# Cross-attention of sample tokens on four 32-column groups of the array, with eight cache slots

## The chip, the cores and the metric

The kernel runs on one core of one Trainium2 chip, all in float32 or float32r. The metric is the time of one execution on the device, in microseconds (us). TensorE is called PE here, VectorE DVE, ScalarE ACT, GpSimd POOL and SyncE SP.

## The reference

One layer of an encoder over 1024 prompt tokens (one sequence) and 8 x 16 sample tokens. The change touches the cross-attention of the sample tokens: each of the eight sequences has keys and values of its own, 256 memory tokens by four heads of 256.

```python
def mem_attention(q, mk, mv):
    s = jnp.einsum('bthd,bmhd->bhtm', q, mk.astype(q.dtype)).astype(jnp.float32) * (XA_DH ** -0.5)
    p = jax.nn.softmax(s, axis=-1).astype(q.dtype)
    return jnp.einsum('bhtm,bmhd->bthd', p, mv.astype(q.dtype))

def layer(x, ml_state, conv_buf, mk, mv, ...):
    xn = rms_norm(x, g_mix_pre)
    q, k, v, o, ig, fg, glu, xq, gates = jnp.split(xn @ w_in, IN_SPLITS, axis=-1)
    ...
    y_xa = mem_attention(xq.reshape(B, T, XA_HEADS, XA_DH), mk, mv).reshape(B, T, XA_W)
    mixed = (jax.nn.sigmoid(gates[..., 0:D_MODEL]) * (y_ml @ w_branch[0])
             + jax.nn.sigmoid(gates[..., D_MODEL:2 * D_MODEL]) * (y_cv @ w_branch[1])
             + jax.nn.sigmoid(gates[..., 2 * D_MODEL:]) * (y_xa @ w_branch[2]))
    x = x + rms_norm(mixed @ w_out, g_mix_post)
    ...
```

In the kernel the sample tokens are the last of nine tiles of 128 tokens: `mem_attention` runs on eight prompt tiles with one set of keys, then on the sample tile with eight.

## The kernel before, in words

The program is a sequence of phases, each written once for every engine: norms, the input projection, the projection of the convolution's branch, the mLSTM and its branch, the cross-attention (`sp_xattn`, `pe_xattn`, `act_xattn`, `dve_xattn`, `pool_xattn`) and its branch, and the FFN. Each engine runs its own list in order and waits on semaphores. Barrier 4 (`end_phase`) stands ahead of the cross-attention. The projection after it (L261, `pe_branch(pe, 2, xa_lo, 2 * NT)`) waits until POOL has written `A_lo` of all nine tiles (L1690).

Prompt tiles: for tile t PE computes scores (L1531, stationary queries, moving keys `mk_T`, two PSUM banks), DVE the maxima (L1701), ACT the exponentials with row sums (L1632), DVE scales by the reciprocal (L1708), PE transposes the probabilities (L1541), ACT copies them to `prob_T` (L1640), and PE multiplies with `mv` (L1550). SP loads the queries two tiles ahead (L1497), when the scores of the tile two before are done.

Sample tile, keys. The keys of sample b are loaded as rows of memory tokens into one of four slots of `cache_in` (L1484), so PE turns them by 16 transposes (`k_turn`, L1586) into four PSUM banks. ACT copies two of the banks (L1668) and DVE the other two (L1746) to one of two buffers `ck_T`, which lie on `mk_T` and `mv`. Then `k_scores` (L1596) multiplies: for each of 8 pieces of 128 columns the stationary operand is `xqm`, 128 columns of queries of which only the 16 of sample b are not zero, and the moving operand 256 columns of keys. All samples add into the same 128 x 1024 scores, head by head in columns. DVE makes `xqm` for each sample, by a clear (L1740) and a small copy (L1742).

```python
for k in range(KT):
    h = k // 2
    last = nc.tensor.matmul(PS[:, h // 2, MEM * (h % 2):MEM * (h % 2 + 1)], xqm[:, s, k], ck_T[s][:, k],
                            start=first and k % 4 == 0, stop=end and k % 4 == 3, skip_group_check=True)
```

Softmax of the sample tile: as for a prompt tile (L1701, L1632, L1708, L1541, L1640).

Sample tile, values. DVE makes for each sample a stationary operand `prob_own` (L1766 or L1764 clears, L1767 copies), again with 16 of 128 columns that are not zero, and PE multiplies it with the values of that sample (L1617), 8 matmuls of 256 moving columns. Then ACT copies the result (L1682), PE transposes it (L1623), DVE halves it into `xa_T` (L1717), ACT rounds it to `A_hi` (L1646) and POOL takes the rest to `A_lo` (L1690).

Loads. SP issues the keys of samples 0 to 3 behind the last query load, each later one when its slot has been turned; of the values SP issues samples 0, 2, 4, 6 and ACT 1, 3, 5, 7, each when its slot is free (`values`). Elsewhere the normaliser update of the mLSTM uses a stationary operand of 8 columns (L1256), which the prediction reads for comparison; L1252 ahead of it is full width.

## Time and profile before

| what | value |
|---|---|
| median of 3 runs | 2808.9 us (2807.84 to 2810.91) |
| the profiled execution, its time | 2810.57 us |
| the profiled execution, its span (first to last instruction) | 2808.8 us |
| mean granted clock of PE | 0.985 of 2.4 GHz |
| prompt tiles of the cross-attention | 1602.67 to 1673.5 us |
| keys, softmax, values of the sample tile | 1673.5 to 1755.0 us |
| first instruction of the projection behind it | 1761.45 us |

The profile is of one execution. Times in it count from the start of the span. "PE" rows are matmuls; "PEld" rows are loads of the stationary operand, which overlap them. A record of PE is longer than the distance to the next, since matmuls are pipelined: the distance from start to start is what one costs in a stream. A form such as 128\*8 128x256 says: 128 partitions by 8 stationary columns, 256 moving columns.

### The profile page before, as it was taken

Reading aid. Unit: us, or ns where it says so; the run is one execution under the profiler, and the core shown is the slowest. Engines: PE = TensorE matmul, PEld = TensorE weight load, DVE = VectorE, ACT = ScalarE, POOL = GpSimd, SP = SyncE. Lnnn points to the kernel's source line nnn. Section 1 sums busy time; section 2 is a strip of 40 time slices with the busy share of each in tenths; the row PEclk is TensorE's granted clock in tenths of the full one; section 3 lists DMA queues with packets and bytes.
Section 4 is the critical chain, followed back from the end, with each engine's and each line's share of the span. In section 5 each row is a group of like instructions: output and inputs, shape, how many; then the busy total and the mean of one; then the engine's idle time right before and its main releaser. Section 6 shows DMA issues by size and latency. Waiting matters only on the chain.

```text
span 2808.8 us, 37457 instructions
## 1 busy us (share of the span) xinstructions
PE 2686.7 (96%) x15080; PEld 2566.7 (91%) x15080; DVE 1087.8 (39%) x1334; ACT 625.3 (22%) x912; POOL 650.2 (23%) x332
## 2 busy tenths in 40 slices
PE   5899999999999999899998898999999999999998
PEld 5899999999999999898888887988999998989897
DVE  3320199999962222216643342245220211110115
ACT  4331111111113233204521141024211110201021
POOL 5421212222221211221201120140313231404131
PEclk9999999999999999999999999999999999999999
DMA  6422333334252223244565534442202020202013
GB/s 180 144 88 88 106 129 121 110 108 142 91 186 80 96 79 105 98 160 106 135 209 177 175 130 147 163 137 90 75 23 68 29 63 23 68 16 68 13 40 135
DMA packets 286828, 294.96 MB, mean 105 GB/s; under 512 B 11386, under 2 KB 250322, under 8 KB 286704
## 3 DMA queue, kind: packets, MB, share of 16 engines
q1 hardware_dynamic: 271800, 239.91, 27.6%
q10 hardware_dynamic: 14912, 53.48, 4.8%
q8 instruction: 75, 1.23, 0.2%
q14 instruction: 41, 0.34, 0.0%
HBM read 208.27 MB, written 85.55 MB: 105 GB/s over the span
## 4 chain that ended last, share of the span: by engine, by line
PE 49%; issue 39%; POOL 8%; DVE 2%; ACT 1%; DMA 1%; SPq 0%; POOLq 0%; DVEq 0%; ACTq 0%
PE PS L1966 19%; PE PS L261 11%; PE PS L1989 9%; POOL w_lo L253 7%; PE PS L1936 3%; PE PS L1531 1%; PE PS L1550 1%; PE PS L1206 1%; PE PS L1214 1%; PE PS L1172 1%; DVE x_T L536 0%; PE PS L1179 0%; DVE y_T L1369 0%; DMA stage<-in_state_conv 0%; PE PS L1167 0%
## 5 line engine op out<-in xcount | busy, mean ns | idle before, releaser
L261 PE MATMUL PS<-A_hi,w_hi 128*128 128x384 f32 x2496 | 573.4, 336 | 17.3 <-DVE A_lo L935 10.0
L261 PE MATMUL PS<-A_lo,w_hi 128*128 128x384 f32 x2496 | 570.9, 335 | 0.0
L261 PE MATMUL PS<-A_hi,w_lo 128*128 128x384 f32 x2496 | 570.4, 335 | 0.0
L253 POOL TENSOR_TENSOR w_lo<-w_raw,w_hi 128x1024 fp32r<-128x1024 f32 x120 | 306.1, 2554 | 1052.6 <-ACT w_hi L249 1052.6
L261 PEld LDWEIGHTS PS<-A_hi,w_hi 128*128 128x128 f32 x2496 | 446.4, 188 | 20.1 <-issue 17.0
L261 PEld LDWEIGHTS PS<-A_lo,w_hi 128*128 128x128 f32 x2496 | 446.5, 188 | 0.0
L261 PEld LDWEIGHTS PS<-A_hi,w_lo 128*128 128x128 f32 x2496 | 446.2, 188 | 0.0
L890 DVE SCALAR_TENSOR_TENSOR c_out<-ext,taps,c_out 128x1024 f32<-128x1024 f32 x480 | 424.1, 962 | 0.7 <-DVE c_out L890 0.7
L249 ACT CAST w_hi<-w_raw 128x1024 fp32r<-128x1024 f32 x120 | 126.3, 1053 | 1079.2 <-PE PS L261 1071.8
L1966 PE MATMUL PS<-A_hi,w_hi 128*128 128x384 f32 x1056 | 242.5, 334 | 2.8 <-POOL w_lo L1881 2.8
L1966 PE MATMUL PS<-A_lo,w_hi 128*128 128x384 f32 x1056 | 242.3, 334 | 0.0
L1966 PE MATMUL PS<-A_hi,w_lo 128*128 128x384 f32 x1056 | 242.2, 334 | 0.0
L1966 PEld LDWEIGHTS PS<-A_hi,w_hi 128*128 128x128 f32 x1056 | 188.2, 188 | 3.5 <-POOL w_lo L1881 3.1
L1966 PEld LDWEIGHTS PS<-A_lo,w_hi 128*128 128x128 f32 x1056 | 188.4, 188 | 0.0
L1966 PEld LDWEIGHTS PS<-A_hi,w_lo 128*128 128x128 f32 x1056 | 188.4, 188 | 0.0
L1881 POOL TENSOR_TENSOR fo_lo<-w_raw,fo_hi 128x1024 fp32r<-128x1024 f32 x22 | 52.9, 2404 | 412.9 <-ACT fo_hi L1876 412.9
L1881 POOL TENSOR_TENSOR w_lo<-w_raw,w_hi 128x1024 fp32r<-128x1024 f32 x44 | 106.2, 2415 | 151.4 <-ACT w_hi L1876 151.4
L2162 DVE SCALAR_TENSOR_TENSOR vb<-vb,PS 128x1152 f32<-128x1152 f32 x22 | 29.8, 1354 | 272.8 <-ACT vb L2043 272.8
L1989 PE MATMUL PS<-fo_hi,G_hi 128*128 128x512 f32 x396 | 122.7, 391 | 0.0
L1989 PE MATMUL PS<-fo_lo,G_hi 128*128 128x512 f32 x396 | 122.0, 389 | 0.0
L1989 PE MATMUL PS<-fo_hi,G_lo 128*128 128x512 f32 x396 | 122.0, 389 | 0.0
L2173 DVE TENSOR_TENSOR Y_tok<-Y_tok,PS 128x1024 f32<-128x1024 f32 x45 | 54.9, 1221 | 153.6 <-PE PS L1989 153.0
(289 smaller groups left out, 2766.3 us busy)
## 6 DMA issues: line engine op xcount, KB each, us to landing
proj_d<-stage ACTq DMA_DIRECT2D x80, 576.0 KB, 2.7
w_raw<-in_w_in SPq DMA_DIRECT2D x80, 512.0 KB, 4.2
w_raw<-in_w_ffn_in SPq DMA_DIRECT2D x44, 512.0 KB, 3.9
w_raw<-in_w_branch SPq DMA_DIRECT2D x24, 512.0 KB, 4.3
w_raw<-in_w_ffn_out SPq DMA_DIRECT2D x22, 512.0 KB, 3.4
glu<-proj_d SPq DMA_DIRECT2D x16, 576.0 KB, 5.9
gate_in<-proj_d SPq DMA_DIRECT2D x16, 576.0 KB, 6.4
part_d<-part_out SPq DMA_DIRECT2D x16, 576.0 KB, 4.7
```

What stands on the lines that cost most here:

```text
L249: nc.scalar.copy(w_hi[:, s % SPLIT, 0:kt], w_raw[:, s, 0:kt]).then_inc(w_hi_done, 1)
L253: nc.gpsimd.tensor_tensor(w_lo[:, s % SPLIT, 0:kt], w_raw[:, s, 0:kt], w_hi[:, s % SPLIT, 0:kt].bitcast(F32), ALU.subtract).then_inc(w_lo_ ...
L261: last = nc.tensor.matmul(out, w[:, k], m(k, c), start=start and k == 0 and n == 0, stop=stop and k == kt - 1 and n == 2)
L890: steps.mark(nc.vector.scalar_tensor_tensor(out=c, in0=src, scalar=tap_scalar(w, k), in1=c, op0=ALU.mult, op1=ALU.add))
L1172: last = nc.tensor.matmul(PS[:, 0, P * h:P * (h + 1)], k_in[:, b, 2 * h + z], q_in[:, b, 2 * h + z], start=z == 0, stop=z == 1)
L1206: last = nc.tensor.matmul(PS[:, 4 + h, 0:E1], q_in[:, b, 2 * h + z], C_T[:, h, z], start=z == 0, stop=z == 1)
L1881: nc.gpsimd.tensor_tensor(l_, job_raw(n), h_.bitcast(F32), ALU.subtract).then_inc(w_lo_done, 1)
L1936: last = nc.tensor.matmul(PS[:, b + z], m_, w_[:, k, 512 * z:512 * (z + 1)], start=k == 0 and n == 0, stop=k == KT - 1 and n == 2)
L1966: last = nc.tensor.matmul(PS[:, 3 * (u % 2) + c, 0:TC], w_[:, u % 2, k], m_[:, k, TC * c:TC * (c + 1)], start=k == 0 and n == 0, stop=k == ...
L1989: last = nc.tensor.matmul(PS[:, b + z], g_[:, k, P * t:P * (t + 1)], w_[:, k, 512 * z:512 * (z + 1)], start=k == 0 and n == 0, stop=k == C ...
L2162: nc.vector.scalar_tensor_tensor(out=thirds(vb[:]), in0=thirds(vb[:]), scalar=1.0, in1=PS[:, 0:3, 0:TC], op0=ALU.add, op1=ALU.mult).then_i ...
L2173: nc.vector.tensor_tensor(Y_tok[:, t], Y_tok[:, t], pair(fo_banks(t)), ALU.add).then_inc(y_acc, 1)
```

## The change

Rows and columns of the sample tile's scores are laid out anew. Before, row 16b + r was token r of sample b, and the columns held the four heads. Now the row is 32h + 16e + r for head h and sample 2p + e, and the columns hold the four pairs p of samples, 256 for each. A matmul for sample b and head h has 32 stationary columns, of which 16 are zero (those of the other sample of the pair), and writes PSUM partitions 32h to 32h + 31; the program gives it the array tile of 128 rows by 32 columns at column 32h. In the order of the program, heads take turns.

- `own_q`, the queries of all eight samples, lies over both buffers of `prob_T` and is made once, by a clear of 2048 columns (L1719 of the changed kernel) and two copies. `own_p`, the probabilities, lies over both buffers of `prob` and is made once, by a clear of 2048 columns (L1734) and four copies (L1738).
- There are eight slots for keys and values: four of `cache_in` and four new ones (`cache_more`). Key b is loaded behind the query load of prompt tile b + 2, so during the prompt tiles. Value b is loaded into slot b when its keys have been turned, all by SP.
- The loops over samples are written out. The last transposes and the halving follow the new layout.
- Semaphores of the mLSTM phase are used again, so POOL clears them before barrier 4 instead of behind it.

```diff
-        cache_loaded = [sem(f"cache_loaded{s}") for s in range(4)]
...
+        ml_sems.close()
+        cache_loaded = [sem(f"cache_loaded{s}") for s in range(NB)]
...
-        prob_own = prob[:].rearrange("p b h m -> p b (h m)").rearrange("p b (m h j) -> p b m h j", m=2, h=H)
+        own_q = prob_T[:].rearrange("p a m h j -> p (a m h j)").rearrange("p (b k r) -> p b k r", b=NB, k=KT)
+        own_p = prob[:].rearrange("p b h m -> p (b h m)").rearrange("p (m b h r) -> p m b h r", m=2, b=NB, h=H)
...
+        cache_more = [nc.alloc_sbuf_tensor_at(f"cache_more{n}", [P, 2, D], F32, offset=x) for n, x in enumerate((201600, 209792, 217984, O_GATE))]
...
         def sp_xattn(sp):
...
+            for t in range(2, NPT + 1):
+                load_xq(sp, t, t % 2)
+                cache(sp, "cache_mem_k", t - 2)
+            cache(sp, "cache_mem_k", NB - 1)
+            for b in range(NB):
+                sp.wait_ge(ck_turn, 2 * (b + 1))
+                cache(sp, "cache_mem_v", b)
...
+            def k_scores(b):
                 pe.wait_ge(ck_a, b + 1)
                 pe.wait_ge(ck_d, b + 1)
-                pe.wait_ge(ck_q, b + 1)
-                for k in range(KT):
-                    h = k // 2
-                    last = nc.tensor.matmul(PS[:, h // 2, MEM * (h % 2):MEM * (h % 2 + 1)], xqm[:, s, k], ck_T[s][:, k],
-                                            start=first and k % 4 == 0, stop=end and k % 4 == 3, skip_group_check=True)
+                pe.wait_ge(ck_q, 1)
+                p = b // 2
+                for z in range(2):
+                    for h in range(H):
+                        last = nc.tensor.matmul(PS[32 * h:32 * (h + 1), p // 2, MEM * (p % 2):MEM * (p % 2 + 1)], own_q[:, b, 2 * h + z],
+                                                ck_T[b % 2][:, 2 * h + z], start=b % 4 == 0 and z == 0, stop=b % 4 == 3 and z == 1,
+                                                skip_group_check=True)
                 last.then_inc(ck_used, 1)
...
+            pe.wait_ge(cv_own, 1)
             for b in range(NB):
-                pe.wait_ge(cv_own, b + 1)
-                pe.wait_ge(cache_loaded[b % 4], 16 * (NB // 4 + b // 4 + 1))
...
+                pe.wait_ge(cache_loaded[b], 32)
+                p = b // 2
+                for m in range(2):
+                    for h in range(H):
+                        last = nc.tensor.matmul(PS[32 * h:32 * (h + 1), 6 + p // 2, DH * (p % 2):DH * (p % 2 + 1)], own_p[:, m, b, h],
+                                                slot_of(b)[:, m, DH * h:DH * (h + 1)], start=b % 4 == 0 and m == 0,
+                                                stop=b % 4 == 3 and m == 1, skip_group_check=True)
                 last.then_inc(cv_used, 1)
...
+            dve.wait_ge(xa_y, NPT)
+            nc.vector.memset(own_q, 0.0).then_inc(sq_zero, 1)
+            dve.wait_ge(sq_zero, 1)
+            for e in range(2):
+                last = nc.vector.tensor_copy(
+                    own_q.rearrange("p (g e) k r -> p g e k r", e=2)[:, :, e, :, TS * e:TS * (e + 1)],
+                    xq_in[:, 0].rearrange("p k (g e r) -> p g e k r", e=2, r=TS)[:, :, e])
+            last.then_inc(ck_q, 1)
...
             dve.wait_ge(xa_copied, SB + 1)
...
+            nc.vector.memset(own_p, 0.0).then_inc(sq_zero, 1)
+            dve.wait_ge(sq_zero, 2)
+            for e in range(2):
+                for m in range(2):
+                    last = nc.vector.tensor_copy(
+                        own_p.rearrange("p m (g e) h r -> p m g e h r", e=2)[:, m, :, e, :, TS * e:TS * (e + 1)],
+                        prob_T[:, 0, m].rearrange("p g (h e r) -> p g h e r", e=2, r=TS)[:, :, :, e])
+            last.then_inc(cv_own, 1)
...
             pool_branch(pool, 1)
+            clear_mlstm(pool)
             end_phase(pool, 4)
-            clear_mlstm(pool)
```

The order of PE's instructions at the end of the keys, the softmax and the values, before (the last rows of the loop over samples, then what follows; "x64" is 64 matmuls of the program; the shape is that of the output):

```order
L1586 MATMUL PS<-ident,cache_in 128x128 x16
L1596 MATMUL PS<-mk_T,prob_T 128x256 x8
L1603 REGISTER_ALU
L1603 COMPARE_AND_BRANCH
L1596 MATMUL PS<-mv,prob_T 128x256 x8
L1541 MATMUL PS<-ident,prob 128x128 x8
L1617 MATMUL PS<-cache_in,prob 128x256 x64
L1623 MATMUL PS<-ident,prob_T 128x128 x8
```

and in the changed kernel:

```order
L1574 MATMUL PS<-ident,cache_more_54 128x128 x16
L1585 MATMUL PS<-mk_T,prob_T 32x256 x8
L1585 MATMUL PS<-mv,prob_T 32x256 x8
L1529 MATMUL PS<-ident,prob 128x128 x8
L1604 MATMUL PS<-cache_in,prob 32x256 x32
L1604 MATMUL PS<-cache_more_51,prob 32x256 x8
L1604 MATMUL PS<-cache_more_52,prob 32x256 x8
L1604 MATMUL PS<-cache_more_53,prob 32x256 x8
L1604 MATMUL PS<-cache_more_54,prob 32x256 x8
L1611 MATMUL PS<-ident,prob_T 128x128 x8
```

The matmuls are as many as before and stand in the same places; each writes 32 partitions, not 128.

The order of DVE's instructions from the last sample's key copy to the last halving, before:

```order
L1746 COPY mv<-PS 128x1024
L1751 REGISTER_ALU
L1751 COMPARE_AND_BRANCH
L1701 TENSOR_REDUCE smax<-PS 128x4
L1706 RECIPROCAL rsum<-ssum 128x4
L1708 TENSOR_SCALAR prob<-prob,rsum 128x256 x4
L1766 MEMSET prob 128x1024
L1767 COPY prob<-prob_T 128x8x16
L1766 MEMSET prob 128x1024
L1767 COPY prob<-prob_T 128x8x16
L1764 MEMSET prob 128x8x16
L1767 COPY prob<-prob_T 128x8x16
```

and in the changed kernel:

```order
L1730 COPY mv<-PS 128x1024
L1681 TENSOR_REDUCE smax<-PS 128x4
L1686 RECIPROCAL rsum<-ssum 128x4
L1688 TENSOR_SCALAR prob<-prob,rsum 128x256 x4
L1734 MEMSET prob 128x2048
L1738 COPY prob<-prob_T 128x4x4x16 x4
L1746 TENSOR_SCALAR xa_T<-PS 128x2x128 x4
```

All eight operands are now made ahead of the first value matmul, where one was.

The order of SP's transfers around the cross-attention, before:

```order
L1497 DMA xq_in<-proj_d 128x8x128 [waits xa_S]
L1484 DMA cache_in<-in_cache_mem_k 128x2x1024 x4
L1515 UNCONDITIONAL_BRANCH
L1484 DMA cache_in<-in_cache_mem_k 128x2x1024 [waits ck_turn] x4
L1515 REGISTER_ALU
L1515 COMPARE_AND_BRANCH
L1484 DMA cache_in<-in_cache_mem_v 128x2x1024 [waits ck_turn] x2
L1484 DMA cache_in<-in_cache_mem_v 128x2x1024 [waits cv_used] x2
```

and in the changed kernel:

```order
L1494 DMA xq_in<-proj_d 128x8x128 [waits xa_S]
L1489 DMA cache_more_52<-in_cache_mem_k 128x2x1024
L1494 DMA xq_in<-proj_d 128x8x128 [waits xa_S]
L1489 DMA cache_more_53<-in_cache_mem_k 128x2x1024
L1489 DMA cache_more_54<-in_cache_mem_k 128x2x1024
L1489 DMA cache_in<-in_cache_mem_v 128x2x1024 [waits ck_turn] x4
L1489 DMA cache_more_51<-in_cache_mem_v 128x2x1024 [waits ck_turn]
L1489 DMA cache_more_52<-in_cache_mem_v 128x2x1024 [waits ck_turn]
```

Key loads now alternate with the query loads, and no value load waits for a value matmul.

## Rows read from the trace of the kernel before

**Rows 1.** The page, busy time and share of the span by engine.

```profile
PE 2686.7 (96%) x15080; PEld 2566.7 (91%) x15080; DVE 1087.8 (39%) x1334; ACT 625.3 (22%) x912; POOL 650.2 (23%) x332
```

**Rows 2.** Windows by stretch: us, busy of each engine (instructions), clock, DMA share, GB/s.

```profile
1608.00:1649.60 41.60, 40.25 (x271) 36.93 (x270) 20.52 (x45) 20.99 (x61) 9.71 (x8) 1.00 0.27 77
1649.60:1673.50 23.90, 20.62 (x164) 19.41 (x162) 9.72 (x20) 10.80 (x26) 7.96 (x7) 1.00 0.51 198
1673.50:1716.10 42.60, 42.18 (x256) 37.85 (x256) 19.11 (x26) 8.77 (x10) 2.52 (x2) 1.00 0.56 198
1716.10:1725.40 9.30, 2.01 (x9) 1.64 (x9) 3.69 (x8) 2.94 (x9) 0.00 (x0) 0.64 0.00 0
1725.40:1755.00 29.60, 29.58 (x128) 25.41 (x128) 3.49 (x14) 0.00 (x0) 0.00 (x0) 0.94 0.41 142
1755.00:1761.50 6.50, 1.14 (x9) 0.91 (x9) 1.29 (x2) 2.23 (x3) 2.48 (x2) 0.86 0.00 0
```

**Rows 3.** Groups by line and shape, 1673.5 to 1761.4 us: busy, mean ns | idle before.

```profile
L1617 PE MATMUL PS<-cache_in,prob 128*128 128x256 f32 x128 | 29.6, 396 | 2.6 <-issue 2.6
...
L1586 PE MATMUL PS<-ident,cache_in 128*128 128x128 f32 x128 | 15.5, 274 | 1.7 <-DVE xa_T L1717 1.4 <-ACT mk_T L1668 0.3
L1596 PE MATMUL PS<-mk_T,prob_T 128*128 128x256 f32 x64 | 14.5, 379 | 0.0
...
L1746 DVE COPY mv<-PS 128x1024 f32<-128x1024 f32 x4 | 4.9, 1223 | 0.3
```

**Rows 4.** Timeline of PE in the keys: start us, us, engine, line.

```profile
1677.78 3.62 PE L1596 MATMUL PS<-mk_T,prob_T 128*128 128x256 f32 x16
...
1681.23 1.91 PE L1586 MATMUL PS<-ident,cache_in 128*128 128x128 f32 x16
...
1682.98 3.62 PE L1596 MATMUL PS<-mv,prob_T 128*128 128x256 f32 x16
```

**Rows 5.** Timeline of the softmax of the sample tile and the first value operand.

```profile
1719.59 1.14 DVE L1708 TENSOR_SCALAR prob<-prob,rsum 128x256 f32<-128x256 f32 x4
...
1724.08 0.91 DVE L1766 MEMSET prob<- 128x1024 f32 x1 [3.35 <-ACT prob_T L1640]
1725.03 0.23 DVE L1767 COPY prob<-prob_T 128x128 f32<-128x128 f32 x1
```

**Rows 6.** Timeline of PE in the last normaliser update of the mLSTM.

```profile
1478.85 1.03 PE L1252 MATMUL PS<-Cb_T,qm 128*128 128x257 f32 x4
1479.81 1.89 PE L1256 MATMUL PS<-kw,own 128*8 128x256 f32 x8
```

**Rows 7.** Windows of two us at the start of the values, PE alone.

```profile
1726.00:1728.00 2.00, 2.00 (x6) 0.50 0.00 0
1728.00:1730.00 2.00, 2.00 (x9) 0.77 0.00 0
```

**Rows 8.** DMA: windows of a query load and of key loads; landing of four key loads.

```profile
1624.00:1632.00 8.00, 8.00 (x58) 7.54 (x57) 3.75 (x8) 4.06 (x11) 2.59 (x3) 1.00 0.24 68
1656.00:1664.00 8.00, 7.51 (x61) 6.94 (x61) 3.81 (x8) 4.37 (x12) 2.64 (x3) 1.00 0.82 338
...
DMA to landing us min/median/max: 6.2/9.0/11.9
DMA to landing us min/median/max: 3.9/4.1/9.0
```

**Rows 9.** Timeline of DVE at the end of the prompt tiles.

```profile
1673.67 0.91 DVE L1740 MEMSET prob_T<- 128x1024 f32 x1 [0.16 <-issue]
...
1674.62 0.51 DVE L1742 COPY prob_T<-xq_in 128x128 f32<-128x128 f32 x1
...
1675.57 1.23 DVE L1746 COPY mk_T<-PS 128x1024 f32<-128x1024 f32 x1 [0.44 <-PE PS L1586]
```

**Rows 10.** Timeline of a prompt tile: query loads and scores.

```profile
1608.22 41.35 SPq L1497 DMA_DIRECT2D xq_in<-proj_d  x7
...
1613.78 3.62 PE L1531 MATMUL PS<-mk_T,xq_in 128*128 128x256 f32 x16
```

More of the change, by code:

```diff
@@ L1603, in pe_xattn @@
-            with pe.Fori(1, NB // 4) as i:
-                for s in range(4):
-                    b = 4 * i + s
-                    k_turn(b, s, i)
-                    k_scores(b - 1, 1 - s % 2)
-            k_scores(NB - 1, 1, end=True)
+                pe.wait_ge(ck_q, 1)
[5 more added lines that the diff above has]
+                                                skip_group_check=True)
@@ L1609, in pe_xattn @@
+                last.then_inc(ck_used, 1)
+            k_turn(0)
+            for b in range(1, NB):
+                k_turn(b)
+                k_scores(b - 1)
+            k_scores(NB - 1)
+            pe.wait_ge(ck_a, NB)
             p_turn(SB, 0)
             pe.wait_ge(xa_copied, SB + 1)
+            pe.wait_ge(ck_d, NB)
+            pe.wait_ge(cv_own, 1)
             for b in range(NB):
-                pe.wait_ge(cv_own, b + 1)
-                pe.wait_ge(cache_loaded[b % 4], 16 * (NB // 4 + b // 4 + 1))
@@ L1615, in pe_xattn @@
-                for h in range(H):
-                    for m in range(2):
-                        last = nc.tensor.matmul(PS[:, 6 + h // 2, DH * (h % 2):DH * (h % 2 + 1)], prob_own[:, b % 2, m, h],
-                                                cache_in[:, b % 4, m, DH * h:DH * (h + 1)], start=b == 0 and m == 0 and h % 2 == 0,
-                                                stop=b == NB - 1 and m == 1 and h % 2 == 1, skip_group_check=True)
+                pe.wait_ge(cache_loaded[b], 32)
+                p = b // 2
@@ L1662, in act_xattn @@
             hi(NPT - 1)
-            def keys(b, s):
+            for b in range(NB):
                 act.wait_ge(ck_turn, 2 * b + 1)
-                if not isinstance(b, int) or b > 1:
+                if b > 1:
                     act.wait_ge(ck_used, b - 1)
-                nc.scalar.copy(ck_T[s][:, 0:4].rearrange("p (a k) m -> p a (k m)", a=2), PS[:, 4:6]).then_inc(ck_a, 1)
-            keys(0, 0)
-            keys(1, 1)
-            with act.Fori(1, NB // 2) as i:
-                for s in range(2):
-                    keys(2 * i + s, s)
-            for b in (1, 3):
-                values(act, b)
+                nc.scalar.copy(ck_T[b % 2][:, 0:4].rearrange("p (a k) m -> p a (k m)", a=2), PS[:, 4:6]).then_inc(ck_a, 1)
             act.wait_ge(ck_used, NB)
@@ L1678, in act_xattn @@
             turned(SB, 0)
-            for b in (5, 7):
-                values(act, b)
             act.wait_ge(cv_used, NB)
+            act.wait_ge(cv_own, 1)
             nc.scalar.copy(xa_nat, PS[:, 6:8].rearrange("p n c -> p (n c)")).then_inc(cv_nat, 1)
@@ L1759, in dve_xattn @@
             dve.wait_ge(xa_copied, SB + 1)
[L1760 to L1768 removed]
+            nc.vector.memset(own_p, 0.0).then_inc(sq_zero, 1)
[6 more added lines that the diff above has]
+            last.then_inc(cv_own, 1)
+            dve.wait_ge(cv_turned, 1)
+            for n in range(2):
+                dve.wait_ge(xa_lo, 2 * SB + n - 1)
+                for z in range(2):
+                    last = nc.vector.tensor_scalar(xa_T[:, n].rearrange("p (h z) (g r) -> p z h g r", z=2, r=32)[:, z],
+                                                   PS[:, 6 + z].rearrange("p (g h r) -> p h g r", h=H, r=32)[:, 2 * n:2 * n + 2], 0.5, None, ALU.mult)
+                last.then_inc(xa_half, 1)
         early_sems.close()
[L1772 removed]
         U_F = U_BR + 3 * KT
```

86 lines of the change are left out of this document (19 added, 67 removed).

## The prediction

> **What bounds it now.** I read the page first: PE is busy 96% of the span [rows 1], so what counts is where PE works longer than it must, or waits. The windows then cut the cross-attention into stretches [rows 2]: eight prompt tiles (1608 to 1673.5), the keys of the eight samples (1673.5 to 1716.1), the softmax of the sample tile (to 1725.4), the values (to 1755.0) and the way back to the next projection (to 1761.5). Keys and values take 42.6 + 29.6 us, and PE is busy in 42.18 and 29.58 of them, so both stretches end when PE ends, and DVE and ACT are covered there. In the softmax stretch PE works 2.01 of 9.3 us: there each DVE and ACT step is on the path.
>
> The groups by line say what PE does [rows 3]. A sample's keys are 16 transposes and 8 score matmuls, its values 8 matmuls. 64 score matmuls stand as 2 x 64 records (one group for each buffer of keys; one is shown) and 64 value matmuls as 128: an f32 matmul goes through the array in two passes. In the timeline [rows 4] one sample's 16 passes run from 1677.78 to the next instruction at 1681.23: 3.45 us, 216 ns a pass, and the 16 transposes from 1681.23 to 1682.98: 1.75 us. So keys cost 5.2 us and values 3.46 us a sample, whatever share of the 128 stationary columns is zero.
>
> **The array.** Each matmul now has 32 stationary columns and writes partitions 32h to 32h + 31; the count stays 8 + 8 a sample with 256 moving columns each. The nearest rows are the eight passes of L1256, with 8 stationary columns [rows 6]: 1.89 us from first start to last end, 7 x 216 + 379 ns. A narrow matmul alone is therefore not shorter; all gain must come from passes in different column groups that run at once. No row here shows two passes at once, so the bounds are 16 slots of 216 ns a sample (none overlaps) and 4 slots (all four groups at once). I take the middle, 8 slots: the two passes of one matmul have the same 32 columns and follow one another in the stream, so the second has to wait for the first; if passes start in program order, what can overlap is the second pass of head h with the first pass of head h + 1, two at a time.
> - Values: 128 passes in 64 slots, 13.8 us in place of 27.65: **13.8 gained**.
> - Keys: 8 slots and one for the last lone pass are 1.94 us in place of 3.46.
>
> The Trainium skill, "TensorE: Matmul & The Clock Gate", part 3 on packing small matmuls, says that matmuls stay in program order and that three column tiles at once measured 2.38 times as fast; no run so far shows it here. By that figure alone the 55.3 us of scores and values would fall to an estimated 23 us, between my middle and the lower bound.
>
> **Changes of array shape.** Full-width transposes and narrow matmuls alternate in the keys, 14 changes that cost anything. The trace has the change: the last of four L1252 passes starts 3 x 216 ns after 1478.85, at 1479.50, the next was due at 1479.72 and came at 1479.81 [rows 6]: 0.1 us. Bounds are nothing and 163 ns (the 379 of a record less the slot of 216). I take 0.1: 1.4 us. The Trainium skill, "TensorEngine Tiling (Array Packing)", key properties, says that a change of tiling mode drains TensorE; the 0.1 us gap agrees.
>
> **Keys, put together.** At the end of the prompt tiles DVE cleared 1024 columns (0.91 us), copied 128 queries, and was idle till the first keys came at 1675.57 [rows 9]. Now it clears 2048 (1.82) and makes two copies of 512. A four-pack of 256-column operations runs in 1.14 us [rows 5], 0.285 each, so I take 0.57 a copy. The first key copy then starts at 1673.67 + 1.82 + 1.14 + 0.1 = 1676.7, 1.1 us late, and the second half of the next transposes waits for it: the first scores start at 1677.78 + 1.1 + 0.1 = 1679.0. From there 8 x 1.94 + 6 x 1.75 + 1.4 = 27.4 us, end 1706.4 instead of 1716.1: **9.7 gained**. The six other clears and small copies that leave DVE were covered by PE; they gain nothing. DVE's key copy of 1.22 us [rows 3] has 1.94 + 0.87 us of PE beside it. If scores took 0.87 us, DVE would be nearly level, which costs 0.4 us once, at the last sample.
>
> **Softmax.** The same instructions up to prob_T. Then a clear of 0.91 and a copy of 0.23 [rows 5] stood before the first value matmul; now it is a clear of 2048 columns (1.82) and four copies of 256 (4 x 0.285 = 1.14, between 4 x 0.23 and 4 x 0.35): **1.9 lost**, since PE waits for the last copy. The seven later operand builds ran beside 3.46 us of PE each and gain nothing. The halving at the end is four operations of 256 columns for two of 512: **0.1 lost**.
>
> **Clock.** PE idles in the softmax, and its granted clock falls to 0.50 (1.2 GHz); the first values run so until about 1729.5, when it returns to 1.0 [rows 7]. Values took 29.6 us for 27.65 of work, so the fall costs 2 us. PE idles there as before or longer, so the same 2 us stays, in each case below.
>
> **Loads.** Each key load of 1 MB now goes behind a query load on SP's queue, one per prompt tile. A query tile takes 0.24 of 8 us, 1.9 us of the engines; at 338 GB/s the share was 0.82, so 1 MB takes about 2.6 us. 4.5 us a tile stand against 7.9. Four key loads issued together landed after 6.2 to 11.9 us [rows 8], one after the other, so a query load waits for one key load at most, 2.6 us on top of its 4.1. From the third prompt tile on it has over 7 us to spare (issue at the end of the tile two before); the one for tile 2, issued at 1608.2, lands before the first key load: PE wanted it at 1613.78 [rows 10]. Nothing, at worst 1 us. Value loads are issued at each sample's transposes, the last near 1703, and needed from 1718: hidden. The four that ACT issued move to SP, which waits for nothing else there. POOL's clear of semaphores is done before the barrier, while SP still waits for stores: nothing.
>
> **Sum.** 9.7 + 13.8 - 1.9 - 0.1 = 21.5 us. The profiled execution took 2810.57 us (its span is 2808.8), 1.7 above the median of the runs; 2810.57 - 21.5 = 2789.1, and against the median of 2808.9 it is **2787.4 us**. Its own range, with the change of shape at 0 to 163 ns and an overlap somewhat better or worse than pairs, is 2782 to 2794.
>
> **Rivals.**
> - *All four groups at once.* Scores 0.87 us a sample: 7.0 + 10.5 + 1.4 + 0.4 from 1679.0 is 1698.3, 17.8 gained; values 6.9 for 27.65, 20.7 gained; less 2.0: 36.5, **2772.4 us**. For it: the heads stand in turn in the stream. Against: each stands there as two passes of one group. The 2.38 of the page named above lies on this side. 15%.
> - *No overlap.* Keys 8 x 3.46 + 10.5 + 1.4 = 39.6 from 1679.0, 2.5 lost; values even; 2.0 lost in softmax and end: 4.5 lost, **2813.4 us**, 0.16%. For it: no row shows two passes at once, L1256 least of all, though its passes are of one group. 20%.
> - *Slower: a change of column group costs like a change of shape.* Passes do not overlap and each of the 128 matmuls goes to another group than the one before; at the 0.1 us of rows 6 that is 12.8 us more: **2826 us**. It decides from 10 ns a change on (1.2 us over 128). Against: at full width each pass takes another stationary operand, and its 216 ns are 256 columns at two cycles of 2.4 GHz (213 ns) with no room for such a cost [rows 4]. 10%.
> - *Late queries.* The key loads delay each of seven query loads so that a tile waits 2 us: 14 us given back, **2801 us**. Against: 4.5 of 7.9 us. 5%.
>
> **How the numbers follow.** Pairs 47%, four 15%, none 20%, slower 10%, late queries 5%, the rest mixtures. About 0.2%, 5.6 us, is what a measurement can tell from no change. Faster 0.70; without overlap the loss is so near 0.2% that its 20% is split: same 0.16, slower 0.14. Pairs and four hold 62%, so the range must reach to no overlap as well: 2770 to 2815.
>
> **What would show it.** Right: value passes 108 ns apart on average, a sample's scores 1.9 us, the values over in 16 us with the first 4 us at half clock; first scores 1.2 us later than before; a clear of 1.8 us before the values. Wrong: passes still 216 ns apart (no overlap), 54 ns (four), PE idle between samples with DVE or a load named, query waits in the prompt tiles, or a stretch of 7.9 us a tile that has grown.

## The result, and the profile after

The changed kernel takes **2778.1 us** (median of 4 runs, 2776.85 to 2779.18) against 2808.4 for the kernel before in 4 runs of the same session: a ratio of 0.989, 95% interval 0.9873 to 0.9907. The profiled execution took 2779.18 us (span 2777.4), 31.4 less than that of before. The forecast was 2787.4, with 2770 to 2815: the direction and the range hold, the size does not, for 21.5 us were forecast.

The page, busy time and share of the span by engine, answers to [rows 1]:

```profile
PE 2652.0 (95%) x15080; PEld 2530.1 (91%) x15080; DVE 1079.7 (39%) x1312; ACT 624.9 (23%) x912; POOL 648.7 (23%) x332
```

PE has the same 15080 instructions and 34.7 us less busy time. The windows by stretch, with the columns of [rows 2], say where:

```profile
1608.00:1649.60 41.60, 40.24 (x271) 36.93 (x270) 20.54 (x45) 20.98 (x61) 9.78 (x8) 1.00 0.65 228
1649.60:1673.50 23.90, 20.59 (x164) 19.38 (x162) 9.70 (x20) 10.82 (x26) 7.95 (x7) 1.00 0.30 110
1673.50:1699.00 25.50, 23.58 (x256) 17.24 (x256) 12.69 (x11) 8.74 (x10) 2.54 (x2) 1.00 0.83 301
1699.00:1710.20 11.20, 1.94 (x9) 1.60 (x10) 5.21 (x11) 2.94 (x9) 0.00 (x0) 0.64 0.17 68
1710.20:1720.00 9.80, 9.80 (x128) 5.41 (x128) 0.00 (x0) 0.00 (x0) 0.00 (x0) 0.72 0.01 2
1720.00:1726.60 6.60, 1.13 (x12) 0.89 (x9) 1.42 (x4) 2.25 (x3) 2.48 (x2) 0.95 0.00 0
```

| stretch | before | after | gained | forecast |
|---|---|---|---|---|
| keys | 42.6 | 25.5 | 17.1 | 9.7 |
| softmax | 9.3 | 11.2 | -1.9 | -1.9 |
| values | 29.6 | 9.8 | 19.8 | 13.8 |
| way back | 6.5 | 6.6 | -0.1 | -0.1 |

Together 34.9 us, 3.5 more than the whole program gained. The timeline of after, all engines, in the keys and from the softmax on (start, duration, engine, line):

```profile
1673.54 1.97 PE L1574 MATMUL PS<-ident,cache_in 128*128 128x128 f32 x16 [1.38 <-DVE xa_T L1697]
1673.86 1.76 DVE L1719 MEMSET prob_T<- 128x2048 f32 x1 [0.38 <-issue]
...
1675.65 1.22 DVE L1722 COPY prob_T<-xq_in 128x512 f32<-128x512 f32 x2
...
1678.06 1.09 PE L1574 MATMUL PS<-ident,cache_in 128*128 128x128 f32 x8 [1.17 <-DVE mk_T L1730]
1679.08 1.07 PE L1585 MATMUL PS<-mk_T,prob_T 128*32 128x256 f32 x16
...
1680.09 1.97 PE L1574 MATMUL PS<-ident,cache_in 128*128 128x128 f32 x16
...
1699.03 1.23 DVE L1681 TENSOR_REDUCE smax<-PS 128x4 f32<-128x1024 f32 x1 [1.23 <-PE PS L1585]
...
1707.24 1.76 DVE L1734 MEMSET prob<- 128x2048 f32 x1 [3.58 <-ACT prob_T L1628]
1709.04 0.90 DVE L1738 COPY prob<-prob_T 128x256 f32<-128x256 f32 x4
1710.20 6.36 PE L1604 MATMUL PS<-cache_in,prob 128*32 128x256 f32 x64 [4.50 <-DVE prob L1738]
1716.37 3.64 PE L1604 MATMUL PS<-cache_more,prob 128*32 128x256 f32 x64
```

A sample's 16 score passes take 1.01 us (1679.08 to 1680.09) where they took 3.45 [rows 4]. Full-clock values take 3.64 us for 64 passes, 54 ns a pass and the tail of the last. The windows of a few hundredths of a microsecond on the scores of sample 0 show how (PE, passes in flight in parentheses):

```profile
1679.06:1679.08 0.02, 0.00 (x0) 1.00 2.98 1229
1679.08:1679.10 0.02, 0.02 (x3) 1.00 1.49 614
1679.10:1679.20 0.10, 0.10 (x4) 1.00 0.60 246
...
1679.28:1679.32 0.04, 0.04 (x4) 1.00 0.00 0
1679.32:1679.40 0.08, 0.08 (x8) 1.00 1.37 563
```

Four passes start within 20 to 30 ns of one another, and the next four some 0.24 us after them, while the first four run out; from then on each group starts a pass every 216 ns. **All four column groups run at once.**

What was lost behind the cross-attention is mostly TensorE's clock. The first instructions after the same wait for `w_lo` in the FFN, first in the timeline of before, then in that of after:

```profile
2003.17 0.81 PE L1966 MATMUL PS<-A_hi,w_hi 128*128 128x384 f32 x3 [2.78 <-POOL w_lo L1881]
```

```profile
1968.95 1.33 PE L1945 MATMUL PS<-A_hi,w_hi 128*128 128x384 f32 x3 [2.78 <-POOL w_lo L1860]
```

PE was idle 2.78 us in both; in before the granted clock stayed at 1.00, in after it fell. Windows of two us, PE alone: before behind that wait, then after at the start of the values and behind the wait:

```profile
2003.17:2005.17 2.00, 2.00 (x11) 1.00 0.76 225
```

```profile
1714.00:1716.00 2.00, 2.00 (x28) 0.57 0.03 8
...
1970.00:1972.00 2.00, 2.00 (x8) 0.50 0.87 254
```

From that instruction to the end of the span before takes 805.6 us (2808.8 - 2003.17) and after 808.4 (2777.4 - 1968.95): 2.8 of the 3.5 us. The other 0.7 lie between the first L261 and that wait (241.7 against 242.4). That is one execution of each kernel: the medians are 30.3 us apart, and which clock the other executions had there is not recorded.

### The profile page after: what moved, and what is told of

Read it like the earlier page. It is cut to its first block, busy times and chain, and to the rows that moved or that the text cites. A ratio compares the mean times of both kernels' runs of the same rounds, so it can differ in the third digit from the quotient of the medians.

```text
span 2777.4 us, 37366 instructions
## 1 busy us (share of the span) xinstructions
PE 2652.0 (95%) x15080; PEld 2530.1 (91%) x15080; DVE 1079.7 (39%) x1312; ACT 624.9 (23%) x912; POOL 648.7 (23%) x332
## 4 chain that ended last, share of the span: by engine, by line
PE 50%; issue 38%; POOL 8%; DVE 2%; ACT 1%; DMA 1%; SPq 0%; POOLq 0%; DVEq 0%; ACTq 0%
PE PS L1945 20%; PE PS L261 11%; PE PS L1968 10%; POOL w_lo L253 7%; PE PS L1915 3%; PE PS L1519 1%; PE PS L1538 1%; PE PS L1206 1%; PE PS L1214 1%; PE PS L1172 1%; DVE x_T L536 0%; PE PS L1179 0%; DMA stage<-in_state_conv 0%; DVE y_T L1369 0%; PE PS L1167 0%
## 5 line engine op out<-in xcount | busy, mean ns | idle before, releaser
L261 PE MATMUL PS<-A_hi,w_hi 128*128 128x384 f32 x2496 | 574.0, 336 | 17.6 <-DVE A_lo L935 10.0
L261 PE MATMUL PS<-A_lo,w_hi 128*128 128x384 f32 x2496 | 571.6, 335 | 0.0
L261 PE MATMUL PS<-A_hi,w_lo 128*128 128x384 f32 x2496 | 571.5, 335 | 0.0
L261 PEld LDWEIGHTS PS<-A_hi,w_hi 128*128 128x128 f32 x2496 | 447.2, 189 | 20.2 <-issue 17.1
L261 PEld LDWEIGHTS PS<-A_hi,w_lo 128*128 128x128 f32 x2496 | 447.2, 189 | 0.0
L261 PEld LDWEIGHTS PS<-A_lo,w_hi 128*128 128x128 f32 x2496 | 447.0, 189 | 0.0
```

The costliest lines, as they stand in the source:

```text
L261: last = nc.tensor.matmul(out, w[:, k], m(k, c), start=start and k == 0 and n == 0, stop=stop and k == kt - 1 and n == 2)
```

## How the runs are compared

The start of the cross-attention wanders: the wait for the first queries ends up to 3 us earlier or later by run. The clock behind the FFN wait differs too. So beside the time stands a **stretch**: from the first key transposes (1673.54 in after) to the first L261 (1726.58). The stretch and the clock are those of the profiled execution, in us; the ratio is against the kernel before in the same session, whose median there was 2808.4 to 2810.7. So medians of different sessions can differ by some 2 us without a reason in the kernel, and 2778.1 is of another session than the runs below:

| kernel | median | ratio, 95% | stretch | clock behind the FFN wait |
|---|---|---|---|---|
| before | 2808.4 | | 87.9 | stays |
| after | 2778.1 | 0.989, 0.9873 to 0.9907 | 53.0 | falls |
| one_head_in_a_row | 2776.75 | 0.988, 0.9863 to 0.9896 | 53.2 | falls |
| one_group | 2816.55 | 1.0026, 1.0017 to 1.0036 | 93.9 | falls |
| two_groups | 2789.68 | 0.993, 0.9913 to 0.9946 | 66.3 | falls |
| late_keys | 2777.03 | 0.9887, 0.987 to 0.9903 | 52.9 | stays |
| four_slots | 2783.96 | 0.9904, 0.9889 to 0.9919 | 61.7 | stays |
| eight_in_a_row | 2781.29 | 0.9895, 0.9875 to 0.9914 | 60.8 | stays |
| sixteen_in_a_row | 2788.81 | 0.9923, 0.9904 to 0.9941 | 67.7 | stays |
| thirtytwo_in_a_row | 2792.76 | 0.9937, 0.9918 to 0.9955 | 71.0 | stays |
| early_operands | 2773.85 | 0.987, 0.9855 to 0.9885 | 49.6 | falls |
| early_and_busy | 2765.96 | 0.9842, 0.9829 to 0.9855 | 46.0 | falls |
| busy_more | 2763.41 | 0.9833, 0.982 to 0.9846 | 46.0 | stays (0.56 us of wait left) |
| before_busy | 2807.55 | 0.999, 0.998 to 0.9999 | 85.3 | falls |

A fall of the clock there costs 1.3 to 2.8 us and comes with kernels of any order, so a difference of 3 us between two profiled executions says nothing without that column, and one of 3 us between two medians little.

## Experiments: is it the column groups?

The theory after the result: the gain is the overlap of different column groups and nothing else. Against it stood that narrow operands are cheaper by themselves, and that the overlap needs the heads in turn in the stream.

**One column group.** Every head goes to partitions 0 to 31.

```diff
-nc.tensor.matmul(PS[32 * h:32 * (h + 1), p // 2, ...], own_q[:, b, 2 * h + z], ...)
+nc.tensor.matmul(PS[0:32, p // 2, ...], own_q[:, b, 2 * h + z], ...)
...
-nc.tensor.matmul(PS[32 * h:32 * (h + 1), 6 + p // 2, ...], own_p[:, m, b, h], ...)
+nc.tensor.matmul(PS[0:32, 6 + p // 2, ...], own_p[:, m, b, h], ...)
```

> The changed kernel with the score and value matmuls of all heads writing partitions 0 to 31, column group 0; the output of the sample tile's cross-attention is then not the reference's, and the same instructions run otherwise. Theory A: still 1.07 us a sample, 2778 us. Theories B and C: 216 ns a pass, 3.46 us a sample in scores and in values, 2.6 us more in 16 places, 41 us, less about 1 us of half clock hidden: 2819 us. That is also the time of everything in the change but the overlap: if it is over the 2808 us of the kernel before, the rest of the change costs time, by my sum about 4.5 us.

Its timeline of PE:

```profile
1677.08 3.64 PE L1585 MATMUL PS<-mk_T,prob_T 128*32 128x256 f32 x16
1680.65 1.97 PE L1574 MATMUL PS<-ident,cache_in 128*128 128x128 f32 x16
...
1728.18 16.93 PE L1604 MATMUL PS<-cache_in,prob 128*32 128x256 f32 x64 [4.49 <-DVE prob L1738]
1744.94 13.98 PE L1604 MATMUL PS<-cache_more,prob 128*32 128x256 f32 x64
```

A sample's scores take 3.57 us again, 216 ns a pass, and the values 30.7. The whole gain is gone, and the stretch is 6.0 us longer than in before: a narrow pass of one group is worth nothing, and this is the "no overlap" case that I had priced at 4.5 us. (With one group or two, heads write over one another and the sample tile's attention comes out different; the instructions are the same.)

**Two column groups** (`h % 2` in place of `h` in both outputs: `PS[32 * (h % 2):32 * (h % 2 + 1), ...]`).

> The changed kernel with heads 0 and 2 in column group 0 and heads 1 and 3 in group 1; the output of the sample tile's cross-attention is then not the reference's. Theory A: no change, 2778 us. Theory B: two passes at once, 8 slots of 216 ns a sample, 1.73 us, 0.86 us more in 16 places: 14 us more, 2792 us. Theory C: the second pass of one head beside the first of the next, also 8 slots, 2792 us. If four passes start together even here, B and C fall.

```profile
1676.70 1.92 PE L1585 MATMUL PS<-mk_T,prob_T 128*32 128x256 f32 x16
...
1723.79 7.09 PE L1604 MATMUL PS<-cache_more,prob 128*32 128x256 f32 x64
```

At full clock 64 value passes take 7.09 us with two groups, 13.98 with one and 3.64 with four. Less the tail of the last pass (379 - 216 = 0.16 us) that is 6.93, 13.82 and 3.48: **2.0 and 4.0 times as fast**. This run also draws what my likeliest case would have looked like: scores of 1.9 us a sample and a stretch of 66.3.

**One head in a row.** The loops over `h` and over the two halves change places, so that one group gets four passes in a row, not two.

```diff
-for z in range(2):
-    for h in range(H):
+for h in range(H):
+    for z in range(2):
...
-for m in range(2):
-    for h in range(H):
+for h in range(H):
+    for m in range(2):
```

> The changed kernel with the two inner loops swapped, so that both matmuls of a head, four passes of one column group, follow one another. The changed kernel shows four passes starting within 20 ns and 16 passes of a sample in 1.07 us. Theory A (any four narrow passes in a row run at once, whatever their groups): no change, a sample's scores in 1.07 us, 2778 us. Theory B (one pass at a time in each group, but a group's next pass may overtake passes of other groups in the stream by some places): no change if it looks 12 passes ahead, up to theory C's time if it looks less far. Theory C (one pass at a time in each group, passes start strictly in program order): only the last pass of a head overlaps the first of the next, 13 slots of 216 ns a sample, 2.8 us; 9 slots more than now in 16 places, 31 us more, 2809 us.

The stretch is 53.2 against 53.0, a sample's scores stand as 1.09 us for 16 passes, the values take 9.8. Four passes in a row of one group cost next to nothing (1.09 for 1.07). So the groups do not have to stand in strict turn, and the question became how far ahead the stream reaches.

## Experiments: how far ahead the stream reaches

The values' loops, with 4 samples of one head in a row (16 passes of one group), 8 samples (32 passes) and 2 samples (8 passes):

```diff
-for m in range(2):
-    for h in range(H):
-        last = nc.tensor.matmul(...)
+for g in range(NB // 4):
+    for h in range(H):
+        for b in range(4 * g, 4 * (g + 1)):
+            for m in range(2):
+                last = nc.tensor.matmul(...)
```

> The changed kernel with the value matmuls in another order: for four samples at a time, all 16 passes of head 0 (group 0), then the 16 of head 1, and so on. With 4 passes of a group in a row four still ran at once, so passes overtake others that wait for their group, by at least 12 places. Theory B1 (it looks at least 48 places ahead): values in 9.8 us as in the changed kernel, of which the first 5.6 at half clock. Theory B2 (it looks 12 to 47 places ahead): groups start one after the other and overlap in part; at 16 places two groups run at once, 64 slots of 216 ns, 13.8 us at full clock, about 17 with the start at half clock. Theory C2 (no overtaking beyond what was seen): 61 slots of 64 in each half, 26 us, 29 with half clock.

The values run from 1707.79 to about 1732.3, 24.5 us. Where one head ends and the next begins the records interleave. The timeline of PE at the only border at which the buffer's name changes as well:

```profile
1720.80 0.40 PE L1606 MATMUL PS<-cache_more,prob 128*32 128x256 f32 x1
1721.01 0.38 PE L1606 MATMUL PS<-cache_in,prob 128*32 128x256 f32 x1
1721.04 0.38 PE L1606 MATMUL PS<-cache_more,prob 128*32 128x256 f32 x1
1721.22 0.38 PE L1606 MATMUL PS<-cache_in,prob 128*32 128x256 f32 x1
1721.25 0.38 PE L1606 MATMUL PS<-cache_more,prob 128*32 128x256 f32 x1
1721.44 0.38 PE L1606 MATMUL PS<-cache_in,prob 128*32 128x256 f32 x1
1721.47 10.83 PE L1606 MATMUL PS<-cache_more,prob 128*32 128x256 f32 x61
```

Four passes of the next head (`cache_more`) run beside the last four of the one before (`cache_in`; the first of these, at 1720.79, is not in a row of its own). From this border, and from the 27.9 us of the run of 32, which was made together with it, came the theory: passes are handed out in the order of the stream, each group takes them one at a time, and **a group holds four that run or wait; a fifth stops the stream**, for the other groups too. Each border then saves four slots of 216 ns and no more. The theory was made with both results known; only the run of eight, whose expectation names it, tested it ahead.

> The same for all eight samples: 32 passes of each group in a row. B1 with a reach of 96 places or more: 9.8 us. With a reach of 48 to 95 places two or three groups overlap: 14 to 19 us. With a reach under 32 places: nearly one after the other, 25 us or more. The time against the run with 16 in a row tells the reach.

> The value matmuls for two samples at a time, 8 passes of each group in a row. Theory D, made after the runs with 16 and 32 in a row (24.5 and 27.9 us for the values): passes are handed out in program order, and a group takes up to four of them, running or waiting; only when it holds four does the stream stop. Then with n in a row the next group starts when four passes of this one are left: 128 - 7 x 4 = 100 slots for 16 in a row and 128 - 3 x 4 = 116 for 32, at 0.2165 us and 2.8 us for half clock 24.4 and 27.9 us, as measured; with 4 or 2 in a row nothing stops. For 8 in a row it gives two groups at a time: 64 + 4 = 68 slots, 14.7 + 2.8 = 17.5 us. Rival E (a fixed reach over places of the stream, whatever the groups): a reach that gives four at once with 4 in a row is at least 12 places, which at 8 in a row gives 2 to 2.5 groups at once, 14 to 17 us, but at 16 in a row nearly two, 17 us, against 24.5 measured. D wants 17.2 to 17.8.

The timelines of PE, of 32 in a row at its last border and of 8 in a row over all its values:

```profile
1729.89 0.38 PE L1606 MATMUL PS<-cache_more,prob 128*32 128x256 f32 x1
1729.92 2.97 PE L1606 MATMUL PS<-cache_in,prob 128*32 128x256 f32 x13
1732.73 3.62 PE L1606 MATMUL PS<-cache_more,prob 128*32 128x256 f32 x16
```

```profile
1707.46 9.87 PE L1606 MATMUL PS<-cache_in,prob 128*32 128x256 f32 x61 [4.45 <-issue]
1716.95 0.40 PE L1606 MATMUL PS<-cache_more,prob 128*32 128x256 f32 x1
...
1717.19 0.38 PE L1606 MATMUL PS<-cache_more,prob 128*32 128x256 f32 x1
...
1717.62 7.50 PE L1606 MATMUL PS<-cache_more,prob 128*32 128x256 f32 x61
```

| passes in a row | borders | slots left of 128 | at 216 ns | half clock's cost | sum | measured |
|---|---|---|---|---|---|---|
| 32 | 3 | 116 | 25.1 | 2.6 | 27.8 | 27.9 |
| 16 | 7 | 100 | 21.6 | 2.6 | 24.4 | 24.5 |
| 8 | 15 | 68 | 14.7 | 2.4 | 17.2 | 17.7 |
| 4 | | 32 | 6.9 | 2.7 | 9.7 | 9.8 |
| 2 (after) | | 32 | 6.9 | 2.8 | 9.8 | 9.8 |

Slots left are 128 less four for each border, and never less than a quarter. The half clock's cost is half the time from the first value pass to the rise of the granted clock (4.8 to 5.5 us), and the sum has the tail of the last pass, 0.16 us. The four was read off the runs of sixteen and of 32; the run of eight was forecast with it at 17.2 to 17.8 us and took 17.7. What the sums leave over grows with the borders, 0.1 us for 3 and 7 of them and 0.5 for 15, and the rows name most of it: the second pass of a group that begins comes 0.24 us after its first (1716.95 and 1717.19), not 216 ns, some 0.03 us for each border. A reach of a fixed number of places of the stream, whatever the group, which is the rival E of the last expectation, does not fit: four passes in a row ran at full speed, which takes a reach of 12 places at least, and with such a reach 16 in a row would have taken 17 us, not 24.5. Three or five in place of four would give that run 107 or 93 slots, 25.9 or 22.9 us. In stretch the run of eight stands 7.8 us over after, by the values 7.9. Its profiled execution took only 1.3 us more: it began the keys 2.7 us earlier and kept the clock behind the FFN wait. What stays open is what holds the passes, for no row shows a queue, and whether it is always four: every run here has f32 passes of 256 columns, and four passes are also two matmuls.

The Trainium skill, "TensorE: Matmul & The Clock Gate", part 2 on issuing a matmul, says that matmuls stay in program order. Across column groups the trace does not agree: in the run of sixteen a pass of the next head starts at 1720.80, before the last three of the head ahead of it in the program (1721.01, 1721.22 and 1721.44). Within a group no run shows one out of order, and the theory has only the handing out in order, which no row shows. The 2.38 for three column tiles, which part 3 of that page of the Trainium skill gives, would by an estimate of mine (in proportion to the tiles) be 3.2 times for four; the runs show 4.0 here.

## Experiments: the loads and the slots

**Late keys.** All key loads issued together behind the last query load, into the eight slots.

```diff
     load_xq(sp, t, t % 2)
-    cache(sp, "cache_mem_k", t - 2)
-cache(sp, "cache_mem_k", NB - 1)
+for b in range(NB):
+    cache(sp, "cache_mem_k", b)
```

> The changed kernel with all eight key loads issued behind the last query load, as the first four were before, from 1649.6 us on. 8 MB at 2.6 us a MB take 21 us of the DMA engines, so the last lands near 1672, before the first transposes at 1673.5. Theory: the early key loads hide nothing, no change, 2778 us. Rival: loads land later than their share says (the fourth took 11.9 us before, 2.9 apart), key 7 at 1649.6 + 8 x 2.9 + 3 = 1676, still before its transposes at 1694; the rival gives a loss only if transposes of sample 0 wait, at most 2 us.

Stretch 52.9 against 53.0: **no difference**. (The median is 1.1 lower, within what sessions and the FFN wait's clock do.) Loading keys during the prompt tiles hides nothing here that was not hidden, and costs nothing either.

**Four slots.** Samples 4 to 7 share the slots of 0 to 3, and their loads wait for them.

```diff
-return cache_in[:, b] if b < 4 else cache_more[b - 4]
+return cache_in[:, b % 4]
...
+for b in range(4, NB):
+    sp.wait_ge(ck_turn, 2 * (b - 3))
+    cache(sp, "cache_mem_k", b)
...
-    sp.wait_ge(ck_turn, 2 * (b + 1))
+    if b < 4:
+        sp.wait_ge(ck_turn, 2 * (b + 5))
+    else:
+        sp.wait_ge(cv_used, b - 3)
     cache(sp, "cache_mem_v", b)
```

> The changed kernel with four slots for keys and values instead of eight: keys 0 to 3 still loaded in the prompt tiles, keys 4 to 7 when their slot has been turned, values 0 to 3 when key b + 4 has been turned, values 4 to 7 when value b - 4 has been used. Theory: keys hold (a slot is free 2.9 us x 4 before it is wanted again, against 5 us to landing), but values 4 to 7 are asked for only as the values run, at 0.86 us a sample: value 4 is issued when value 0 is used, lands 5 us later, and the four then come 2.6 us apart instead of 0.43 to 0.86: about 5 + 3 x 2.6 - 3.5 = 9 us more, 2787 us, PE idle before the fifth sample's values with a load as releaser. Rival: transfers are spread so that it costs less than 3 us; then eight slots were not needed.

Its timeline of PE in the last four samples' values:

```profile
1717.16 1.07 PE L1610 MATMUL PS<-cache_in,prob 128*32 128x256 f32 x16 [0.79 <-DMA cache_in<-in_cache_mem_v]
...
1720.94 1.07 PE L1610 MATMUL PS<-cache_in,prob 128*32 128x256 f32 x16 [2.71 <-DMA cache_in<-in_cache_mem_v]
...
1723.39 1.93 PE L1610 MATMUL PS<-cache_in,prob 128*32 128x256 f32 x16 [1.38 <-DMA cache_in<-in_cache_mem_v]
...
1725.82 1.93 PE L1610 MATMUL PS<-cache_in,prob 128*32 128x256 f32 x16 [0.50 <-DMA cache_in<-in_cache_mem_v]
```

PE now needs a sample's values in 0.87 us at full clock, and a load takes longer: it waits for every one of the last four samples, 5.4 us in all, and twice runs at half clock behind such a wait. The stretch is 8.7 us longer, the median 5.9 (in this execution the clock stayed behind the FFN wait). Without the eight slots the values cannot run at the speed of the array.

## Experiments: what the change left on the path

**Early operands.** The queries' operand is built in two halves, the first ahead of the last halving of the prompt tiles; the values' operand lies on `mk_T`, so that its clear runs beside the exponentials.

```diff
-own_p = prob[:].rearrange(...)
+own_p = mk_T[:].rearrange(...)
...
+queries(0)
 half(NPT - 1, xa_y, NPT)
...
-nc.vector.memset(own_q, 0.0)
...
+    if b == 1:
+        queries(1)
...
 maxima(SB, 0, ck_used, NB)
+nc.vector.memset(own_p, 0.0).then_inc(sq_zero, 1)
 norm(SB, 0)
 dve.wait_ge(xa_copied, SB + 1)
-nc.vector.memset(own_p, 0.0).then_inc(sq_zero, 1)
```

> The changed kernel with the operands made earlier: the first half of the queries before the last halving of the prompt tiles, the second half behind the first key copy, and the probabilities' operand laid over the first key buffer and cleared while ACT takes the exponentials. Theory: both clears are on the path in the changed kernel, 1.2 us (the second half of sample 1's transposes waits 1.17 us for DVE) and 1.76 us ahead of the first value; 2.9 us less, 2775.2 us, a first value matmul 9.5 us after the last score instead of 11.2. Rival: the clear delays the maxima or the scaling, and the gain is under 1 us.

Timeline, PE and DVE:

```profile
1696.71 1.23 DVE L1681 TENSOR_REDUCE smax<-PS 128x4 f32<-128x1024 f32 x1 [1.23 <-PE PS L1585]
...
1698.31 1.76 DVE L1735 MEMSET mk_T<- 128x2048 f32 x1 [0.38 <-issue]
...
1705.71 6.33 PE L1604 MATMUL PS<-cache_in,mk_T 128*32 128x256 f32 x64 [2.33 <-DVE mk_T L1741]
```

The stretch is 3.4 us shorter: 1.2 because the first scores no longer wait for DVE's key copy, 2.2 because the clear is off the path (9.0 us from the maxima to the values in place of 11.2). The median falls by 4.3; against the kernel before of its own session it lies 36.6 us lower, where that of after lies 30.3 lower.

**Early and busy.** The same, and PE does 4 + 1 + 4 matmuls that nothing reads around the transposes of the softmax and behind those of the result.

```diff
+def busy(n):
+    for _ in range(n):
+        nc.tensor.matmul(PS[:, 2, 0:512], ident[:], mv[...][:, 0:512], start=True, stop=True)
...
+busy(4)
 p_turn(SB, 0)
+busy(1)
 pe.wait_ge(xa_copied, SB + 1)
...
 last.then_inc(cv_turned, 1)
+busy(4)
```

> The same with matmuls that nobody reads, into a free PSUM bank, while PE waits: four of 512 columns behind the last scores, one behind the transposes of the probabilities, four behind the last transposes. In the changed kernel the granted clock is 0.50 from about 1702 to 1716 and from 1726 to 1732. Theory: half clock costs 0.85 us in the transposes of the probabilities, 2.8 us in the values and about 2.8 us in the next projection; with PE busy the clock stays at 1.00 and 6 us go, 2769 us. Rival: the matmuls themselves delay the real ones, or the clock falls all the same: 2775 us or more.

```profile
1702.56 1.09 PE L1529 MATMUL PS<-ident,prob 128*128 128x128 f32 x8 [1.12 <-DVE prob L1695]
...
1705.89 3.66 PE L1610 MATMUL PS<-cache_in,mk_T 128*32 128x256 f32 x64 [1.38 <-DVE mk_T L1748]
1709.35 3.66 PE L1610 MATMUL PS<-cache_more,mk_T 128*32 128x256 f32 x64
```

Both halves of the values now take 3.66 us, the transposes 1.09 for 1.94 and the stretch is 3.6 us shorter again; the next projection starts at full clock as well, worth 2.9 us up to the FFN wait (239.3 for 242.2). The median is 7.9 under that of early operands, and the kernel is the second fastest of this study. The stretch and the projection make 6.5 us of the 7.9; the traces do not place the rest.

**Busy before.** The same nine matmuls in the kernel before.

> The kernel before with the same unread matmuls as early_and_busy in the softmax stretch and at the end, nothing else. Theory: half clock costs the kernel before as much as the changed one: 1 us in the transposes of the probabilities, 2 us in the values, 2.6 us in the next projection: 5.6 us less than the kernel before, whose column groups have nothing to do with it. Part of the softmax gap after the transposes stays idle for 3.7 us, so the values may still start at half clock: then 3.6 us.

3.1 us less (2807.55 against 2810.67), where more was expected. The values take 27.86 us for 29.62 and the stretch is 2.6 shorter, the branch gives 0.9, and in this run the clock fell behind the FFN wait, which takes 1.3 back. The filling is worth more in the changed kernel: 3.6 us of the stretch and 2.9 of the projection, against 2.6 and 0.9 here.

**Busy more.** The same as early and busy, and 10 small matmuls ahead of the FFN wait, 32 ahead of barrier 4.

```diff
 in_unit(1, (2,), True)
+for _ in range(10):
+    nc.tensor.matmul(PS[:, 7, 0:P], ident[:], ident[:], start=True, stop=True)
...
 pe_branch(pe, 1, ml_lo, 2 * NT + 2)
+for _ in range(32):
+    nc.tensor.matmul(PS[:, 7, 0:P], ident[:], ident[:], start=True, stop=True)
 end_phase(pe, 4)
```

> The kernel early_and_busy with unread matmuls in two more gaps: 32 of 128 columns (7 us) in front of barrier 4, where PE waits 8 us for SP's stores and the clock is at 0.50 for 6.8 us afterwards, and 10 (2.2 us) ahead of the third FFN unit, where PE waits 2.78 us and the clock fell in some executions and not in others. Theory: 3.4 us less at the first gap, 0 to 1.7 at the second (half clock of 3.4 us there in the profile of early_and_busy): 2762 us. Rival: the barrier or the clock does not change, or the matmuls delay the barrier: 2766 or more.

```profile
1592.49 7.31 PE L2292 MATMUL PS<-ident 128*128 128x128 f32 x64
1600.28 3.94 PE L1519 MATMUL PS<-mk_T,xq_in 128*128 128x256 f32 x17 [0.48 <-SPq L271]
```

The first key transposes come 4.1 us earlier than in early and busy (1669.52 for 1673.62). Of this 2.4 us are the clock: from the first scores to the first transposes of the probabilities the first prompt tile takes 8.5 us (1600.28 to 1608.81) for 10.9 (1602.00 to 1612.90). The other 1.7 are the start, which wanders: in eight_in_a_row, without these matmuls, the first scores came at 1600.14. Behind the FFN wait the clock stays up: 805.6 us from there to the end, as in before. Against that, 1.0 us more passes between the first L261 and that place; its cause is open. With a median of 2763.41 against 2809.96 in its session (46.6 us, 1.7%) this is **the fastest version**, 14.7 under the median of the changed kernel.

## Why the prediction was right and wrong

- **That PE bounds keys and values, so that overlap on the array is all the gain:** right. With one group nothing is left of it.
- **"I take the middle, 8 slots":** this step failed. Its reason was that the second pass of a matmul has to wait for the first, and that passes start in program order. The first half is true (one every 216 ns within a group), the second is not: a pass that waits for its group does not hold up those of the next group behind it in the stream, as long as its group holds no more than four. So a sample takes 4 slots and not 8; its scores and the change of shape measure 1.01 us, where I had 1.94 and 0.1. That is rival 1, to which I gave 15%; its working gave 36.5 us, and up to L261 the trace shows 34.9. The nearest rows [rows 6] had a single group and could not tell the two apart; my even middle was a guess about the queue, and the 47% for it too much.
- **The range:** 2778.1 lies in it by luck as far as the mechanism goes. It was drawn from 2770 to 2815 to take in the rivals; the range of the pairs alone, 2782 to 2794, misses it.
- **Shape changes at 0.1 us:** one group measures them alone: 3.57 + 1.89 us a sample for 3.45 + 1.75, 0.13 each. Mis-sized by 0.4 us in all; the keys ended 0.7 us behind rival 1's 1698.3.
- **First scores at 1679.0:** 1679.08, by a clear of 1.76 and two copies in 1.22.
- **Softmax 1.9 lost, halving 0.1:** right as sums (11.2 and 6.6). Inside the 1.9 two errors cancel: the four copies took 0.90 us and not 1.14, and the steps ahead of the clear and the start behind the copies took some 0.4 us more than in before, which stood in no term.
- **"the fall costs 2 us", and "the same 2 us stays":** mis-sized. [rows 7] put the return of the clock at 1728.9, not at 1729.5 (0.77 in the mean of 1728 to 1730), so the fall had cost 1.8. In after the values ran at 0.50 for 5.5 us (1710.2 to about 1715.7), which cost 2.8; PE had idled longer ahead of them, but no run shows that this is the reason. And the clock has a price beyond the stretch that I did not look at: 2.8 us behind the FFN wait. Rival 1's working gave 36.5 us and the profiled executions are 31.4 apart; the 5.1 between are 0.7 in the keys (0.4 by the shape changes), 0.9 in the values (the half clock), 0.7 from L261 to the FFN wait and 2.8 behind it.
- **Loads cost nothing:** right, for the prompt tiles are as long as before and PE as busy in them. But I had not priced what the eight slots are for: without them the values wait for loads, 8.7 us of the stretch.
- **No overlap, 2813.4:** would have come to 2816.5 by the run with one group; the change of column group costs nothing (rival 3 falls: with four groups in turn each still starts a pass every 216 ns). Late queries: no trace of it.

## What to carry to other kernels

When a float32 stationary operand has at most 32 columns that matter and PE is the bound, spread the products over the four column groups: the streams run fully side by side, in whatever order, as long as no more than about four passes of one group follow each other (eight in a row already took 17.7 us for 9.8). Then look at what the faster PE uncovers: loads that need more slots, operand builds on the path, and idle gaps in which the clock falls, where a few matmuls that nothing reads can pay. Compare such variants by a stretch of the trace, since the clock of an unrelated gap moves the total by up to 3 us.

## What the runs showed of the hardware

- Column groups overlap fully, by 2.0 and 4.0 times for two and four groups, with passes of 216 ns each, and changing group costs nothing measurable.
- The times fit a group that holds four passes, running or waiting (f32, 256 columns), and a pass of another group then starts before passes ahead of it in the program; a longer row in one group stops the others: 9.8, 17.7, 24.5 and 27.9 us for rows of up to 4, 8, 16 and 32.
- Behind the same idle gap of 2.76 to 2.79 us in the FFN the granted clock falls in 7 of 13 profiled executions and stays in 6, with the same work around it; in one_group and two_groups it fell only some 1.3 us after PE had started again. A fall cost 1.3 to 2.8 us. No run here says what decides it.
